# Seven-product projections in the attention stage of a fused two-block kernel

## The reference

```python
p, pc = h @ w_in, hc @ w_in                     # tokens and context, both (256, 2048)
q = rms_norm(heads(cols(p, COL_Q)), q_norm_g)   # 16 heads of 128
k, kc = rms_norm(heads(cols(p,  COL_K)), ...), rms_norm(heads(cols(pc, COL_K)), ...)
v, vc = heads(cols(p, COL_V)), heads(cols(pc, COL_V))
ya = neighbourhood_attention(q, k, v, kc, vc, rpb)   # softmax over tokens and context, with a bias table
ya = ya * silu(cols(p, COL_GATE_A))
# then: state-space branch yb, out = concat(ya, yb) @ w_out, a short-convolution layer, a second block
# shift, scale, gate of every layer = silu(c) @ ada_w + ada_b
```

## Time and profile before

| what | value |
|---|---|
| time, median of 3 runs | 2831.66 us (2830.11 to 2832.17) |
| the profiled execution | 2830.7 us, span of the core 2828.5 us |
| PE busy | 2776.7 us (98%) |
| PE weight loads busy | 2235.0 us (79%) |
| DVE busy | 1314.0 us (46%) |
| ACT busy | 441.6 us (16%) |
| POOL busy | 51.4 us (2%) |
| stage na on PE | 136.8 to 930.3 us of the span |
| one iteration of na | 97.4 us |

### The profile page before, as it was taken

How to read it: one execution, slowest core, us unless ns; L and a number is a source line. 1 busy time by engine, 2 the same in 40 slices (tenths; PEclk the granted TensorE clock), 3 DMA queues, 4 the chain that set the end, 5 groups by cost and what they waited for, 6 DMA issues and landing times. The chain is left out here.

```text
span 2828.5 us, 38622 instructions
## 1 busy us (share of the span) xinstructions
PE 2776.7 (98%) x15840; PEld 2235.0 (79%) x15840; DVE 1314.0 (46%) x2317; ACT 441.6 (16%) x867; POOL 51.4 (2%) x72
## 2 busy tenths in 40 slices
PE   7999999999999999999999999999999999999999
PEld 1467866776686566666668888999999899999999
DVE  3643343333243245555555003665666665555543
ACT  0221111111111122222222001111111111121211
POOL 0010000000000000000000000000000000000000
PEclk9999999999999999999999999999999999999999
DMA  9874555655464133333332544555554545545542
GB/s 384 306 248 154 178 170 171 200 181 160 154 202 130 40 105 105 104 104 104 104 104 95 187 150 151 176 166 164 176 169 158 178 134 145 147 150 158 160 139 86
DMA packets 379174, 445.20 MB, mean 157 GB/s; under 512 B 20308, under 2 KB 351560, under 8 KB 378312
## 3 DMA queue, kind: packets, MB, share of 16 engines
q1 hardware_dynamic: 351088, 352.76, 40.6%
q0 software_dynamic: 19520, 75.50, 7.7%
q10 hardware_dynamic: 8472, 15.58, 1.5%
HBM read 439.56 MB, written 4.26 MB: 157 GB/s over the span
## 5 line engine op out<-in xcount | busy, mean ns | idle before, releaser
L529 PE MATMUL bank<-hT,w 128*128 128x128 f32 (+2 forms) x6128 | 1263.4, 365 | 6.1 <-ACT hT L1154 4.6
L529 PEld LDWEIGHTS bank<-hT,w 128*128 128x128 f32 x6128 | 898.2, 193 | 329.8 <-issue 296.1
L529 PE MATMUL bank<-w,hT 128*128 128x256 f32 (+2 forms) x2048 | 394.0, 353 | 0.0
L529 PEld LDWEIGHTS bank<-w,hT 128*128 128x128 f32 x2048 | 350.1, 190 | 48.9 <-issue 10.0
L1154 ACT ACTIVATE work<-bank 128x512 f32<-128x512 f32 (+3 forms) x282 | 146.1, 539 | 1300.3 <-PE bank L529 1295.1
L529 PE MATMUL bank<-yT,w 128*128 128x256 f32 (+1 forms) x1888 | 343.2, 342 | 1.4 <-DVE yT L1870 1.0
L529 PEld LDWEIGHTS bank<-yT,w 128*128 128x128 f32 x1888 | 307.3, 191 | 33.0 <-DVE yT L1870 1.2
L529 PE MATMUL bank<-hT,work 128*128 128x128 f32 x2352 | 279.5, 275 | 0.0
L529 PEld LDWEIGHTS bank<-hT,work 128*128 128x128 f32 x2352 | 270.9, 192 | 0.0
L1701 DVE SCALAR_TENSOR_TENSOR work<-xT,silc,work 128x512 f32<-128x512 f32 x240 | 180.5, 752 | 43.2 <-DMA xT<-in_ada_w 35.2
L1154 ACT ACTIVATE work<-work 128x512 f32<-128x512 f32 (+4 forms) x267 | 150.1, 562 | 245.2 <-DVE work L1767 149.4
(11 more groups left out here) (172 smaller groups left out, 1831.8 us busy)
## 6 DMA issues: line engine op xcount, KB each, us to landing
w<-in_na_ssd_w_in SPq DMA_DIRECT2D x48, 2048.0 KB, 8.4
xT<-in_ada_w POOLq DMA_DIRECT2D x64, 1024.0 KB, 5.6
w<-in_sc_w_in SPq DMA_DIRECT2D x32, 2048.0 KB, 10.3
w<-in_w_in SPq DMA_DIRECT2D x32, 2048.0 KB, 10.4
w<-in_na_ssd_w_out SPq DMA_DIRECT2D x16, 2048.0 KB, 8.4
w<-in_ada_w SPq DMA_DIRECT2D x12, 2048.0 KB, 11.2
w<-in_na_ssd_w_in SPq DMA_DIRECT2D x16, 1024.0 KB, 7.3
w<-in_sc_w_out SPq DMA_DIRECT2D x8, 2048.0 KB, 8.2
```

What stands on the lines that cost most here:

```text
L529: return nc.tensor.matmul(dst, lhsT, rhs, start=start, stop=stop, skip_group_check=free)
```

## The change

Stage na gets the seven-product form for all units but the very first (i = 0, Q). The loops of na are written out instead of being hardware loops. Per iteration:

- PE: `na_unit` does seven products in two parts (four into bank 0, three into bank 1). The third needs t1, the fourth t2, the seventh t4, three sums of the tile's quarters.
- DVE: `sums_one` (two instructions of 128 x 1024 for a tile) makes t1 and one sum in place; `na_combine` puts a unit together (six instructions); `token_sums` runs twice, in iteration 0.
- POOL: `sums_two` makes t2 and t4 of each tile (two `tensor_tensor` of 128 x 1024), at fixed places among its chunk issues.
- ACT: `na_staging` copies the two banks of each unit into one staging buffer, and may start a unit's first copy only when the unit before is combined (`n_made`). Squares and the gate's sigmoid are taken from SBUF, after the combining.
- Weight tiles use three slots in turn instead of four; the fourth holds the sums. Tile n is loaded when tile n - 3 is used up.
- The attention's result goes through `yout` to a scratch in HBM, and comes back to `yT` in stage ssd; token sums of the context lie in `yT` meanwhile.
- The bias tables of the last pair are still loaded behind the two half tiles of ssd's first B and C, which now wait for the slot of the last V tile.

```diff
 # GpSimd
-            for c in range(8):
-                ...
-                wait(gp, late_taken, 8 * i + c - 1)
-                gp.dma_start(aring[:, c % 2, :, :], src).then_inc(late_in[c % 2], 16)
+        def sums_two(n):
+            s, places = na_slot(n), na_places(n)
+            gp.wait_ge(na_t, n)
+            gp.wait_ge(acc_full, na_filled(n - 1, False))
+            nc.gpsimd.tensor_tensor(places[1], quarter(s, 1, 1), places[0], ALU.subtract).then_inc(na_t2, 1)
+            gp.wait_ge(na_t2, 2 * n - 1)
+            nc.gpsimd.tensor_tensor(places[2], quarter(s, 1, 0), places[1], ALU.subtract).then_inc(na_t2, 1)
+        for i in range(8):
+            if i == 0:
+                late_chunk(0, 0)
+                late_chunk(0, 1)
+            sums_two(4 * i + 1)
+            if i > 0:
+                late_chunk(i, 2)
+            sums_two(4 * i + 2)
+            if i == 0:
+                late_chunk(0, 2)
+            sums_two(4 * i + 3)
+            for c in (3, 4, 5):
+                late_chunk(i, c)
+            for c in (6, 7):
+                late_chunk(i, c)
+            if i < 7:
+                late_chunk(i + 1, 0)
+                sums_two(4 * i + 4)
+                late_chunk(i + 1, 1)
 # SyncE
+        for n in range(32):
+            if n < 3:
+                sp.wait_ge(ada_used, 10 + n)
+            else:
+                sp.wait_ge(acc_full, na_filled(n - 3))
+            ...
+            load(na_slot(n), w_in[:, :, at:at + TILE])
+            if n % 4 == 1 and n > 4:
+                na_biases(n // 4 - 1)
+                if phase == "ssd":
+                    return sp.wait_ge(acc_full, na_filled((30, 31, 29)[s]))
 # TensorE
+            product(a(0), quarter(s, 0, 0), x(0, 0), None, turned)
+            product(a(1), quarter(s, 1, 0), x(0, 1), None, turned)
+            ...
+            pe.wait_ge(na_t, n)
+            product(a(2), t1, sums[1], None, turned)
+            pe.wait_ge(na_t2, 2 * n - 1)
+            product(a(3), t2, sums[2], None, turned).then_inc(acc_full, 1)
+            if midway:
+                midway()
+            pe.wait_ge(acc_free, k)
+            product(b(0), quarter(s, 0, 1), sums[3], None, turned)
+            product(b(1), quarter(s, 1, 1), sums[4], None, turned)
+            pe.wait_ge(na_t2, 2 * n)
+            product(b(2), t4, x(1, 1), None, turned).then_inc(acc_full, 1)
 # ScalarE, second half of an iteration
+            for u in (2, 3):
+                na_staging(i, u, 0)
+                na_staging(i, u, 1)
             for ch in range(2):
+                na_square(i, 1 + ch, ksq[:, ch, :], kraw[:, ch, :], 3)
+            if not first:
+                na_store(a)
+            na_sigmoid(i)
+            na_staging(i, 4, 0)
+            na_staging(i, 4, 1)
+            na_rms(i, 1)
+            na_staging(i, 5, 0)
+            na_rms(i, 2)
+            na_staging(i, 5, 1)
 # VectorE, second half of an iteration
+            na_combine(i, 2, kraw[:, :, 0:T])
+            if not first:
                 na_out(a, 0)
                 na_turned(a, 1)
+            late_part(i, 2)
+            late_part(i, 3)
+            na_combine(i, 3, kraw[:, :, T:T + TC])
+            if not first:
                 na_out(a, 1)
+            if i < 7:
+                sums_one(n + 4)
+            late_part(i, 4)
+            late_part(i, 5)
+            na_combine(i, 4, vtok[:, 0:2, :])
             dve.wait_ge(na_ge, i + 1)
+            silu(flat(gsil), flat(graw), flat(gsil)).then_inc(na_g, 1)
+            late_part(i, 6)
+            late_part(i, 7)
             for h in range(2):
                 ...
+            na_combine(i, 5, vtok[:, 2:4, :])
```

More of the change, by code:

```diff
@@ L447, in na_biases @@
                     sp.dma_start(hankel[half * 64:half * 64 + 64, h, :, :], src).then_inc(na_hk_in, 16)
[L449 to L457, removed]
+        for n in range(32):
[3 more added lines that the diff above has]
+                sp.wait_ge(acc_full, na_filled(n - 3))
+            at = (COL_Q, COL_GATE, COL_K, COL_V)[n % 4] + (n // 4) * TILE
+            load(na_slot(n), w_in[:, :, at:at + TILE])
+            if n % 4 == 1 and n > 4:
+                na_biases(n // 4 - 1)
         def ssd(i):
@@ L663, in na @@
             a = i - 1
[L664 to L668, removed]
+            na_unit(i, 0)
             if not first:
                 na_scores(a, 0)
[L671 to L675, removed]
+            na_unit(i, 1)
             if not first:
@@ L678, in na @@
                 na_scores(a, 1)
-            pe.wait_ge(acc_free, BANKS["na"] + 6 * i + 1)
-            wait(pe, na_lnfree, 3 * i)
+                pe.wait_ge(mod_ready, i + 1)
+            na_sums(i, 0, qsq)
+            na_unit(i, 2)
             if not first:
[L683 to L693, removed]
+                na_values(a, 0)
+                na_transposes(a, 1)
+            na_unit(i, 3)
             if not first:
                 na_values(a, 1)
[L696 to L704, removed]
+            na_unit(i, 4)
+            na_sums(i, 1, ksq[:, 0, :])
+            na_unit(i, 5, lambda: na_sums(i, 2, ksq[:, 1, :]))
             late_sums(i)
-        iterations(pe, 8, na)
+        for i in range(8):
+            na(i)
         for h in range(2):
@@ L1208, in _, with shifted @@
         act.wait_ge(mod_ready, 1)
-        for k in range(2):
+        def shifted(k):
             for kc in range(DC):
@@ L1675, in na_out @@
             dve.wait_ge(na_po, 2 * a + h + 1)
-            v.tensor_tensor(chunk(yT, 2 * a + h), bank[5][:, 0:T], gsil[:, h, :], ALU.mult).then_inc(na_y, 1)
+            if h == 0:
+                wait(dve, y_saved, 16 * a)
+            v.tensor_tensor(yout[:, h, :], bank[5][:, 0:T], gsil[:, h, :], ALU.mult).then_inc(na_y, 1)
         def silu(out_, raw, sigmoid):
```

289 lines of the change are left out of this document (188 added, 101 removed).

## The result

| | before | after |
|---|---|---|
| time, median | 2830.89 us (2829.79 to 2832.17, 4 runs) | 2891.28 us (2887.32 to 2892.82, 4 runs) |
| ratio | | 1.0209, interval 1.0195 to 1.0222 |
| span of the profiled execution | 2828.5 us | 2888.8 us |

The change costs 60.4 us. The forecast had the direction (slower) and half of the size (29.3), and the time lies above its range. Three lines of the page of after: busy times of the engines, the granted clock in 40 slices, and the first of POOL's two sums of each tile.

A forecast was written before the change was run, and what follows sets the result against it. PE bounded the kernel before; the chunk chain was expected to bind after. Losses of 2.2 (iteration 0), 13.8 (iterations 1 to 6), 11.8 (iteration 7) and 1.5 (clock behind it) sum to 29.3: 2861 us, range 2800 to 2882.

The forecast's parts named there:

- PE alone: Stage na: a seven-product unit takes 12.5 us, an iteration 89.7, which is 7.8 less, if PE never waits.
- One sum on POOL: POOL's weight sums: 2.45 us each, twice DVE's time, between ends of 1.22 and 4.9.
- The chain binds: POOL's V-tile sums delay chunk 3, then DVE's parts 3 to 7 and the late sums: 91.7 us an iteration before POOL-DVE disturbance.
- chunk 5 ... 8.0 again: In each iteration, chunk 5, sharing with chunk 4 and the bias tables, lands 8.0 us after its issue at 70.2.
- The upper end that I set: Upper end for chunk landings in na: 8.7 and 8.6 us, adding 1.3 us an iteration (10 in all).
- DVE stopped by POOL: Beside part 7, POOL's next-Q-tile sums stop DVE for 4.9 us, making PE wait 5.1; a judgement that decides the sign.
- The first rival: POOL and DVE don't disturb each other beside part 7: 2805 us, faster; chance 0.30.
- The clock: Behind the 5.1 us wait in each iteration PE drops to half clock, losing 3.1 us more.
- Iteration 0: First iteration of na: the same chain without na_out gives 91.6 us against 89.4 before, 2.2 lost.
- One iteration in sum: Iterations 1 to 6: 96.6 us plus 3.1 for the clock, 99.7 against 97.4 before; 13.8 lost in all.
- PE held by ACT: Before U5, ACT copies U4 only after squares, store and sigmoid, at 76.4 against 74.6 wanted; U5 ends at 89.8.
- The tail: End of na: last bias tables wait behind the half tiles, scores start 16.3 us after U5; 11.8 lost, clock 1.5 more.

The follow-up runs named there:

- runs 7: Changed kernel with chunks 3 and 4 issued ahead of POOL's V-tile sums and bias tables behind the next Q tile's load: 2796.14 us, ratio 0.9875.
- run 9: Changed kernel: chunks 3, 4 ahead of V sums, tables behind Q tile, Q-tile sums behind chunk 1, last tables behind last V tile: 2772.52 us.
- run 2: Changed kernel with a pair's bias tables issued behind the next Q tile's load instead of the gate tile's: 2866.14 us, ratio 1.0129.
- run 3: Changed kernel with POOL's sums for the next Q tile moved behind chunk 1 of the next iteration: 2863.26 us, ratio 1.0119.
- run 4: Changed kernel with POOL's two next-Q-tile sums replaced by zero writes over the same blocks: 2863.28 us, ratio 1.0110.
- Run 6: Changed kernel with 22 unread products added on PE ahead of the late sums in iterations 0 to 6: 2871.85 us, ratio 1.0154.
- run 5: Changed kernel with the last pair's bias tables issued behind the last V tile's load, ahead of the half tiles: 2877.19 us, ratio 1.0164.
- run 1: Changed kernel with POOL issuing chunks 3 and 4 ahead of its two sums for the V tile: 2843.02 us, ratio 1.0040.

## Why the prediction was right and wrong, point by point

- **PE alone.** 12.5 us a unit and 89.7 an iteration: 12.5 and 89.76 (runs 7 and 9). Right. Of the 59.8 us by which ssd starts earlier in the trace of run 9, iterations 1 to 6 give 46.1 (forecast for PE alone: 46.8), iteration 0 7.1 (6.5) and iteration 7 with the tail 3.0; the other 3.6 are again a stage na that begins earlier.
- **One sum on POOL.** 2.45 us taken, 2.34 to 2.69 measured for 58 of the 62 sums (the other four, in iteration 0, took 3.2 to 3.4), on the mean 2.42 for the first of a pair and 2.49 for the second. The size is right, though it was a guess between 1.22 and 4.9 with a reason that no run tests. The Trainium skill, "GPSIMD Engine Reference", section 3.1, gives an estimate of 2.25 by half of its figure for 2048 values: the trace is 0.1 us above it at the least, and 0.2 on the mean.
- **The chain binds.** Right, and with it the place of every step. From the start of POOL's sums (54.2 forecast; 601.80 measured) the steps lie so:

| step, us behind POOL's start for the V tile | forecast | after | without the tables (run 2) |
|---|---|---|---|
| part 3 starts | 12.9 | 11.3 | 10.9 |
| part 5 starts | 24.0 | 27.0 | 23.8 |
| part 7 starts | 32.7 | 36.0 | 32.8 |
| part 7 ends | 40.7 | 43.2 | 40.0 |

- **The step that failed** is the size of "chunk 5 ... 8.0 again". Chunk 3, issued at 606.5 ahead of the tables, landed after 6.5 us (1.6 won). Chunk 5, issued at 616.5 while two of the four tables were still being issued, took 12.2; in iteration 0 it took 13.1. The rows before showed a chunk beside a tile's load or beside tables (8.7, 8.6), never beside chunk 4, the store of the attention's result, a tile and the tables together. So the step took 8.0 us for what measured 12.2, and the chain ended 2.5 us later than forecast, with the 1.6 of chunk 3 already won. The upper end that I set, 8.7, was the largest row and not a bound: the change puts into one stretch what the rows show apart. Run 2 shows the tables' part: 2.8 us. That run 2's iteration (100.1 us) comes near the forecast's 99.7 is in part luck: part 3 started 2.0 us earlier than forecast there, and from it to part 5 it was 12.9 us and not 11.1.
- **DVE stopped by POOL.** 4.9 us taken, 7.21 - 3.11 = 4.1 measured here, and up to 4.8 in the other iterations. Right, and it was the judgement on which the sign hung. The first rival (no disturbance, 2805) falls with run 3, which gives 28 us back when only this is taken away, and with run 4. The Trainium skill, "SBUF — State Buffer", section "Who interferes with whom", states that a DVE instruction with two inputs in SBUF contends with a GpSimd instruction that reads SBUF, not with one that only writes it, and that the later one waits fully. The trace agrees, nearly (4.1 us of the 5.1 that POOL's sums take), and run 4 agrees on the writes.
- **The clock.** 3.1 us an iteration taken from one stretch of the trace; the late sums lose 1.7 and the products behind 1.4 to 2.8, 3.2 to 4.5 in all. Run 6 shows it as such (4.0).
- **Iteration 0.** 2.2 us lost by the forecast, 10.5 measured from the stage's own start. The forecast left the late sums' half clock out (1.7). Its chain was longer too: part 7 ended 229.99 - 182.35 = 47.6 us behind POOL's start, not 40.4, with chunk 5 at 13.1 us to landing; that start came 48.8 us into the iteration, near the forecast 49.5.
- **One iteration in sum.** 99.7 forecast. The chain's 2.5, a start of it 0.3 later than forecast at full clock, and 0.9 more of clock make 103.4, which is the measured one. Six times that is 22 of the 31 us that were missing; iteration 0 has 5.1 of the rest (8.3 less the 3.2 of the earlier start), iteration 7 with the tail 3.6.
- **PE held by ACT.** I expected U5 to be up to 1.8 us late behind ACT's squares and sigmoid. Iterations 1 to 6 show one such wait, of 0.66 us, in iteration 2; iteration 0 waits for ACT for 1.98 and 1.81 us around there. Because `late_sums` waited for longer, neither the error nor the waits cost anything.
- **The tail.** Scores 16.3 us behind the end of U5 forecast, 965.26 - 943.63 = 21.6 measured. The mechanism held (run 5 takes the wait away), two sizes didn't: the last table's issue ended 952.78 - 943.63 = 9.2 us behind U5 (forecast 7.4: the four took 6.80 us to issue, in the earlier trace rows 4.25), and the mask began 11.4 us behind that, at 964.20 (forecast 7.9). Again the row that I took has fewer transfers in flight around it; which of them it was, no run shows. The stretch as a whole was only 3.6 us longer than forecast, because U5 ended 89.6 us into iteration 7 and not 92.9, while the part from the scores on took 3.1 us more than before (forecast 1.5).
- **What carried no cost** as said: DVE's new work (52% busy), ACT's pieces, tile loads (11.0 us median landing, two tiles ahead), the way through HBM in its own right. Stage ssd starts 60.0 us later and the span is 60.3 longer, so nothing was lost behind na.
- **The range.** It ended at 2882 by adding small excesses to the chain. The chain goes round in every iteration, with nothing behind it to take up an error in seven of them: 3 us in one landing are 21 us here, as much as the whole reach upwards that I gave it.

What stays open: why chunk 5 took 9.4 us even without the tables; how much of it is chunk 4, how much the gate's tile, how much the store; and why the first sums of POOL in iteration 0 took 3.2 to 3.4 us.

## What to carry to other kernels

A queue of issues on an in-order engine is a pacemaker, so work put between two issues delays the transfer by the wait *of that work for what it needs*, and then everything that the transfer's ring feeds: put the issues first, or the work elsewhere. When a chain's terms come from rows, ask which transfers the change brings together that no row shows together, and let the upper bound be their sum. And where TensorE waits once in each iteration, as here, the wait can cost more than its length: 3.2 to 4.5 us more in clock behind waits of 8.9 to 10.9 us, and much the same behind shorter ones of 3 us. Edits that shorten the wait pay singly for what they shorten, and the clock comes back only when the wait is gone: try them together before dropping any of them.

## What the runs showed of the hardware

- GpSimd's `tensor_tensor` of 128 x 1024 float32 takes 2.34 to 2.69 us (3.2 to 3.4 in four of 62 cases, all in iteration 0), where DVE's takes 1.22. While it ran, DVE's `scalar_tensor_tensor` (128 x 512, two tensors from SBUF) stood: one of them took up to 3.59 us instead of 0.75. Two GpSimd writes of the same blocks, 1.86 us together, cost DVE nothing (run 4).
- Four transfers of 96 KB in rows of 256 bytes took 6.7 us to land in run 2, away from chunks 3 to 5, and 12.7 in the changed kernel, beside a tile, chunks and a store; a 1 MB chunk in their company took 12.2 to 13.1 us, where it took 9.4 with the tables away and 5.6 to 8.7 in the earlier trace rows.
- TensorE's clock after it had stood still before the late sums: these took 3.6 us, twice their time, behind every wait of 2.3 us and more (granted clock 0.50, that is 1.2 GHz) but one, of 4.62 us in run 2, where they took 3.3. Behind waits of 1.75 to 2.2 us they took from 2.1 to 3.5 us in different runs and iterations, and in run 1 the granted clock stood at 0.50 behind them even where they took 2.2. With PE kept at work for 9.66 us in the same place (run 6), they took 1.84 to 1.95 behind a wait of 0.8 us or none, their time at the full clock (2.4 GHz), and in five of seven iterations the products behind them ran at it too.
